# The causal mask of the first attention: an add on VectorE in place of identity products on TensorE

## The reference, cut to what matters

```python
l_own = jnp.einsum('bhqd,bhpd->bhqp', qc, k_own).astype(jnp.float32) * scale
causal = (own0 + kpos_local)[None, :] <= (q0 + qpos_local)[:, None]
l_own = jnp.where(causal, l_own, NEG)
p = jax.nn.softmax(jnp.concatenate([l_sel, l_own], axis=-1), axis=-1)
```

## Time and profile before

| | |
|---|---|
| median of 3 runs | 1293.43 us (1292.57 to 1293.62) |
| the profiled execution: its own time | 1293.48 us |
| its span | 1292.2 us |
| TensorE busy | 1284.3 us, 99% |
| VectorE busy | 938.4 us, 73% |
| ScalarE busy | 723.7 us, 56% |
| granted TensorE clock, mean | 0.999 of full speed |

### The profile page before, as it was taken

One profiled execution on the slowest core, in us unless ns is written; L12 is line 12 of the kernel. 1 busy time (PEld: TensorE's weight loads), 2 busy tenths in 40 slices (PEclk: granted clock), 3 DMA queues, 4 the chain that ended last, 5 costly groups with the idle time before them and its releaser, 6 DMA issues.

```text
span 1292.2 us, 23200 instructions
## 1 busy us (share of the span) xinstructions
PE 1284.3 (99%) x9416; PEld 1172.8 (91%) x9416; DVE 938.4 (73%) x1606; ACT 723.7 (56%) x1265; POOL 91.2 (7%) x181
## 2 busy tenths in 40 slices
PE   9999999999999999999999999999999999999998
PEld 8998999999879999999999999878999888989997
DVE  7866897777877977777877888865677654765553
ACT  7545665556666655557656666653444443744442
POOL 1000000000000000000122233300000000000000
PEclk9999999999999999999999999999999999999999
DMA  8443465553434655544444444456544455465530
GB/s 335 164 163 131 163 228 188 180 188 138 154 104 162 224 199 192 193 166 147 137 143 131 133 117 119 142 189 228 204 172 164 150 192 179 165 243 196 180 147 33
DMA packets 35036, 219.26 MB, mean 170 GB/s; under 512 B 4208, under 2 KB 7664, under 8 KB 9456
## 3 DMA queue, kind: packets, MB, share of 16 engines
q1 hardware_dynamic: 30608, 211.83, 45.3%
q10 hardware_dynamic: 4320, 5.94, 3.0%
HBM read 215.78 MB, written 1.05 MB: 168 GB/s over the span
## 4 chain that ended last, share of the span: by engine, by line
PE 96%; DVE 2%; ACT 1%; issue 1%; POOL 0%; DVEq 0%; ACTq 0%; POOLq 0%
PE bank L328 29%; PE bank L330 28%; PE bank L329 28%; PE bank L720 1%; PE bank L771 1%; PE bank L446 1%; PE bank L1758 1%; PE bank L1775 1%; PE bank L792 1%; PE bank L2449 0%; PE bank L714 0%; PE bank L1914 0%; PE bank L1638 0%; PE bank L582 0%; PE bank L1628 0%
## 5 line engine op out<-in xcount | busy, mean ns | idle before, releaser
L328 PE MATMUL bank<-sb_h_hi,sb_w_hi 128*128 128x256 f32 x1504 | 427.8, 284 | 0.6 <-DVE sb_w_lo L321 0.6
L329 PE MATMUL bank<-sb_h_lo,sb_w_hi 128*128 128x256 f32 x1504 | 420.0, 279 | 0.0
L330 PE MATMUL bank<-sb_h_hi,sb_w_lo 128*128 128x256 f32 x1504 | 419.9, 279 | 0.0
L288 DVE TENSOR_TENSOR sb_w_lo<-sb_raw,sb_w_hi 128x1024 fp32r<-128x1024 f32 x185 | 225.8, 1221 | 96.0 <-ACT sb_w_hi L280 95.6
L328 PEld LDWEIGHTS bank<-sb_h_hi,sb_w_hi 128*128 128x128 f32 x1504 | 282.8, 188 | 4.8 <-issue 2.2
L330 PEld LDWEIGHTS bank<-sb_h_hi,sb_w_lo 128*128 128x128 f32 x1504 | 285.5, 190 | 0.0
L329 PEld LDWEIGHTS bank<-sb_h_lo,sb_w_hi 128*128 128x128 f32 x1504 | 283.0, 188 | 1.6
L280 ACT CAST sb_w_hi<-sb_raw 128x1024 fp32r<-128x1024 f32 x188 | 197.6, 1051 | 94.9 <-PE bank L330 93.1
L291 DVE TENSOR_TENSOR sb_w_lo<-sb_raw,sb_w_hi 128x1024 fp32r<-128x1024 f32 x185 | 226.7, 1225 | 0.0
L281 ACT CAST sb_w_hi<-sb_raw 128x1024 fp32r<-128x1024 f32 x188 | 197.9, 1052 | 0.0
L328 PE MATMUL bank<-sb_w_hi,sb_h_hi 128*128 128x256 f32 (+1 forms) x512 | 160.9, 314 | 0.0
(11 more groups left out here) (382 smaller groups left out, 1940.5 us busy)
## 6 DMA issues: line engine op xcount, KB each, us to landing
sb_raw<-stream SPq DMA_DIRECT2D x199, 1024.0 KB, 4.8
sb_row<-rows ACTq DMA_DIRECT2D x3, 512.0 KB, 3.8
sb_x<-x SPq DMA_DIRECT2D x4, 256.0 KB, 4.6
sb_raw<-stream SPq DMA_DIRECT2D x2, 512.0 KB, 5.8
sb_norm_b<-norm_b ACTq DMA_DIRECT2D x4, 256.0 KB, 4.5
out<-sb_x SPq DMA_DIRECT2D x4, 256.0 KB, 2.0
sb_g_row<-sb_g_rows ACTq DMA_DIRECT2D x7, 128.0 KB, 6.3
sb_retain<-retain ACTq DMA_DIRECT2D x1, 768.0 KB, 4.2
```

Of the source, the lines that this page charges most:

```text
L288: V.tensor_tensor(w_lo[:, b, 0:HALF], raw[:, r, 0:HALF], w_hi[:, b, 0:HALF].bitcast(F32), ALU.subtract).then_inc(lo_done, 1)
L328: T.matmul(out_ap, l_hi, r_hi, start=start, stop=False, **kw)
L329: T.matmul(out_ap, l_hi, r_lo, start=False, stop=False, **kw)
L330: return T.matmul(out_ap, l_lo, r_hi, start=False, stop=stop, **kw)
```

## The change

In the first attention only (`self.grouped` is false there), `scores_pe` no longer issues line 714's four products and no longer waits for `mask_ready`. The first score product of each bank has `start=True` instead. `max_dve` begins with a new function `mask_dve`, which adds the float32 mask in place to the two triangular 128-column blocks of each bank (columns 0 to 127 and 256 to 383, one instruction of 2 x 128 columns per head), and then waits through `chain` for the second of them before the first maximum. The second attention keeps its mask products.

```diff
-                if h0 == 0:
-                    T.wait_ge(mask_ready, 1)
-                for r in range(GH):
-                    T.matmul(bank[3 + r][:, 0:384], ident_b[:], mask_b[:, self.mask_row, :], start=True, stop=False,
-                             skip_group_check=True)
+                if self.grouped:
+                    if g == 0:
+                        T.wait_ge(mask_ready, 1)
+                    for r in range(GH):
+                        T.matmul(bank[3 + r][:, 0:384], ident_b[:], mask_b[:, self.mask_row, :], start=True, stop=False,
+                                 skip_group_check=True)
...
-                                          start=False, stop=a_ == 1, skip_group_check=True)
+                                          start=not self.grouped and a_ == 0 and c0 == 0, stop=a_ == 1,
+                                          skip_group_check=True)
...
+            def mask_dve(self, g, pair):
+                h0 = GH * (self.g0 + g)
+                if h0 == 0:
+                    V.wait_ge(attn_in, 64)
+                for r in pair:
+                    V.wait_ge(scored, h0 + r + 1)
+                    diagonal = bank[3 + r][:, 0:384].rearrange("p (a n) -> p a n", n=P)[:, ::2, :]
+                    causal = masks[:, self.mask_row, :].rearrange("p (a n) -> p a n", n=P)[:, ::2, :]
+                    ins = V.tensor_tensor(diagonal, diagonal, causal, ALU.add)
+                chain(ins)
+
             def max_dve(self, g, pair):
                 h0 = GH * (self.g0 + g)
+                if not self.grouped:
+                    self.mask_dve(g, pair)
                 for r in pair:
                     V.wait_ge(scored, h0 + r + 1)
                     V.reduce_max(small[:, 8 + 2 * r:9 + 2 * r], bank[3 + r][:, 0:P], AX.X)
```

## The result

The changed kernel takes 1295.25 us (median of 20 runs, 1294.57 to 1297.44), the kernel before 1293.09 (median of 20 taken with it). The ratio is 1.0017, with a 95% interval of 1.0011 to 1.0024: 2.2 us slower. By the median that is less than the 0.2% (2.6 us) that was set as the bound of no change; the interval reaches a little beyond it, and leaves no doubt of the sign. 1295.4 was predicted. One of the 20 executions of the kernel before took 1846.47 us, the others 1292.57 to 1293.96; the median doesn't feel it.

A forecast was written before the change was run, and what follows sets the result against it. TensorE, busy 1284.3 of 1292.2 us, was taken as the bound. Over four laps waits of 4.59 us less a saving of 2.64 gave +1.95 on the profiled 1293.48, so 1295.4 us, range 1293.3 to 1297.4.

The forecast's parts named there:

- TensorE's saving: Mask products gone from TensorE ahead of the scores: 0.66 us per lap, 2.64 in four, upper end 0.75 per lap.
- lap one: First attention's first lap: scores 0.66 us sooner, TensorE waits 0.92 - 0.12 = 0.80 at the transposes, net +0.14 us.
- A pair's adds: VectorE's two mask adds for a pair of heads, ahead of the maxima: 0.78 us, low end 0.66, high end 0.96.
- slower rival: VectorE's add in place in PSUM is dearer than a read: at 0.96 us a pair, 1296.9 us; chance 0.24.
- Both pairs count: On VectorE pair A's reciprocal stands behind pair B's scaling, so pair A's probabilities come 0.92 us later.
- Laps two and three dearer: VectorE is not free when scores come sooner: net +0.63 us in lap two, +0.92 in lap three.
- Nothing at pair B: No TensorE wait at the second pair's transposes; in lap two 0.53 us of room shrinks to 0.13.
- The faster rival: The adds are hidden and TensorE keeps its saving of 2.64 us: 1290.8 us; chance 0.04.
- Its second half: Scores going one step ahead on TensorE would give 1.4 us, more than the 0.92 of laps one and four.
- The room: In lap one head 1's probabilities are ready 0.12 us before TensorE's transposes want them.
- Lap two: VectorE idled only 0.17 us, so 0.49 of the saving becomes waiting; TensorE waits 1.29, net +0.63 us.

The follow-up runs named there:

- semaphore experiment: The changed kernel with a semaphore for each add, so each head's first maximum waits for that head's add, not the pair's second; 1294.06 us, ratio 1.0010.
- doubled adds: The changed kernel with the mask adds of each pair done twice; 1304.44 us, ratio 1.0089 against the kernel before.

## Why the prediction was right, point by point

- **TensorE's saving.** Forecast 0.66 a lap. In the changed trace the scores start 0.20 us after the last projection product, as another shape had done in 0.21, and TensorE's shift goes from +0.32 to 34.77 - 35.12 = -0.35 over the removed products: 0.67. Right, but not the whole: the 36 products between scores and transposes are faster too. Their first and last start, in lap one before and then in the changed kernel:

```profile
36.64 0.39 PE L328 MATMUL bank<-sb_h_hi,sb_w_hi 128*128 128x256 f32 x1
40.87 0.28 PE L330 MATMUL bank<-sb_h_hi,sb_w_lo 128*128 128x256 f32 x1
```

```profile
36.30 0.38 PE L328 MATMUL bank<-sb_h_hi,sb_w_hi 128*128 128x256 f32 x1
40.39 0.28 PE L330 MATMUL bank<-sb_h_hi,sb_w_lo 128*128 128x256 f32 x1
```

That is 4.23 us before and 4.09 in the changed kernel. So it is in laps one to three alike, 4.23 with the mask products in the old order (two kernels) and 4.09 to 4.10 without them (all seven); why, no run shows. TensorE thus saves 0.80 us in each of these laps and 0.67 in lap four, 3.1 in all where the forecast has 2.64, and its waits grow by 5.2 where the forecast has 4.59. The net hardly feels it, because a lap with a wait ends when the probabilities come, whenever TensorE got there.
- **A pair's adds.** Forecast 0.78 from the reads of the earlier trace rows, measured 0.80. The doubt was whether a write to PSUM is dearer; it isn't, the adds last 423 ns like the reads of that width, so the slower rival's condition, 0.86, was not met. The 0.90 us that was worked out from the Trainium skill (Perfetto Trace Analysis, Optimizing Scalar/DVE Operations) was too high too. Reads from SBUF are no cheaper here: line 2441 starts at 918.17 and line 2442, which reads SBUF as it does, at 918.51, so 0.34 us where the forecast said 0.33.
- **Both pairs count.** The reciprocal behind pair B's scaling was to move by 1.56 - 0.64. It does: it starts 0.08 us behind the scaling and with no wait for ScalarE, 40.58 - 36.45 = 4.13 us after the first add, where it had been 39.88 - 36.73 = 3.15 after the first maximum. That is 0.98 later, 0.96 by the sum with 0.80 a pair. The semaphore experiment (0.26 to 0.28 us a lap for 0.13 a pair) and the doubled adds (1.5 to 1.6 a lap for 0.80 a pair) confirm it.
- **Laps two and three dearer.** Because VectorE was not free for earlier scores. Leaving the mask out shows it without any add (share of lap three: nothing), moving the weight unit takes it away.
- **Nothing at pair B.** No wait at the second group of transposes in any lap, though only 0.13 us of room was forecast.
- **The faster rival**, that the adds hide, needed room that wasn't there. Its second half was tested: where the scores of lap four do go ahead by a step, the lap keeps its saving. The summary's words on the order of the scores describe what the diff lacks.
- **Off:** lap one by 0.13 us. Of this 0.04 is the 0.80 in place of 0.78, counted twice; and the adds follow the scores' start by 36.45 - 34.77 = 1.68 us where the maxima had followed by 36.73 - 35.12 = 1.61. The other 0.02 is what is left of two terms that nearly cancel. The room was 0.17 us and not 0.12: head 1's transposes started at 41.32 before, the forecast had halved the 0.57 us of the six, which end in a shorter step. And behind a wait the next transpose follows after 0.17 us in place of 0.11, which the forecast lacks. Lap two took 0.08 less than forecast, mostly because its adds could start 0.26 us sooner against TensorE and not only 0.17.
- **Luck in the number.** 1295.4 against 1295.25 is closer than the reading. The forecast was added to an execution of 1293.48 us, 0.4 over the median of 1293.09, and its +1.95 is 0.2 under the 2.16 measured; the two make up for each other. The fair comparison is by laps, +1.95 against +2.03, and there too a saving and waits that were both put too small partly cancel, for the reason given in the first point.

## What to carry to other kernels

On an engine that is busy 99%, the absence of waits is not room: read for each hand-over how long before its use the result is ready, and add the change's delay to that. An operation placed ahead of two pipelined pairs delays the first pair by both, if the first pair's next step stands behind the second pair's work on the same engine. Moving work off the bound engine pays only with the order that covers the receiver's longer chain; here the mask's move is worth -2.5 us or +2.2 us by where the scores, the transposes and one unrelated weight unit stand.

## What the runs showed of the hardware that was not expected

- In a wait of 3.45 us on TensorE the granted clock fell to half (1.2 GHz). The first 5.5 us of products behind the wait ran so, and it cost 2.4 us more than the wait; the waits of 2.3 and 2.6 us in laps one and two of the same kernel cost nothing more, the clock stayed whole there. The Trainium skill (TensorE: Matmul & The Clock Gate, HAM oscillation — how this bites in real kernels) tells of matmuls that run at the lower clock after TensorE has waited too long between bursts. The trace agrees.
- A VectorE add in place in PSUM costs about what a read from PSUM does: 0.34 us from start to start for 256 columns, against 0.33. Waiting for its completion ahead of the next instruction costs 0.12 to 0.13 us more, and nothing if one more instruction stands between.
- Rows of projection products come at two paces, about 0.113 and 0.118 us for 256 columns, in stretches that often last 5 to 15 us. In the prologue they lie in other places in each execution: between 15 and 20 us it is 0.113 in the profile of before and 0.118 in that of the changed kernel, whose code is the same up to there. That is the 0.3 us by which lap one began later. Behind the scores of laps one to three the pace goes with the kernel, as told above. Both paces are at full granted clock; what sets them stays open.
